# Row norms of two inputs from their turned form, and the first pieces of a two-block model in another order

## The reference, cut to what matters

```python
def rms_norm(x, g):
    xf = x.astype(jnp.float32)
    y = xf * lax.rsqrt(jnp.mean(xf * xf, axis=-1, keepdims=True) + EPS)
    return (y * g.astype(jnp.float32)).astype(x.dtype)

mn = rms_norm(mem, mem_norm_g)
mk, mv = jnp.split(mn @ w_mem_kv, 2, axis=-1)      # 2048 x 1024
xn = rms_norm(h, attn_norm_g)
proj = xn @ w_in                                     # 2048 x 6164
```

## Time and profile before

| what | us |
|---|---|
| three timed runs, median | 2530.12 |
| lowest and highest | 2525.76, 2530.87 |
| the profiled execution, its own time | 2527.56 |
| its span in the trace | 2525.5 |

### The profile page before, as it was taken

The page is one execution under the profiler, slowest core; times in us unless marked ns, Lnnn a source line. Parts: engine busy times, 40 slices in busy tenths (PEclk is TensorE's granted clock), DMA queues, the critical chain, the costliest instruction groups (busy, mean ns, idle before and its releaser), DMA issues.

```text
span 2525.5 us, 31458 instructions
## 1 busy us (share of the span) xinstructions
PE 2480.1 (98%) x12038; PEld 2162.5 (86%) x12038; DVE 1551.1 (61%) x1937; ACT 1231.5 (49%) x1585; POOL 80.2 (3%) x67
## 2 busy tenths in 40 slices
PE   8999999999999999999999999999899999999998
PEld 6888888888888888888888778888788888888887
DVE  6585565665656565666555766766655555555557
ACT  6465554544444444445344545565554444444444
POOL 1032120000000000000000000000000000000000
PEclk9999999999999999999999999999999999999999
DMA  9654656666656566656654446675366666666664
GB/s 363 196 167 134 184 191 210 189 201 196 198 198 199 198 199 199 200 196 221 203 180 133 151 140 200 208 265 184 127 206 200 201 201 199 201 200 200 200 201 136
DMA packets 245128, 490.86 MB, mean 194 GB/s; under 512 B 12016, under 2 KB 13328, under 8 KB 244272
## 3 DMA queue, kind: packets, MB, share of 16 engines
q1 hardware_dynamic: 240576, 470.42, 57.7%
q0 software_dynamic: 3888, 16.01, 1.8%
q10 hardware_dynamic: 576, 3.21, 0.3%
HBM read 487.52 MB, written 2.10 MB: 194 GB/s over the span
## 4 chain that ended last, share of the span: by engine, by line
PE 93%; DVE 3%; ACT 2%; DMA 1%; issue 1%; SPq 0%; DVEq 0%; ACTq 0%
PE ps_a L2384 24%; PE ps_a L2386 24%; PE ps_a L2385 24%; PE ps_b L2386 5%; PE ps_b L2384 5%; PE ps_b L2385 5%; DMA raw<-in_w_mem_kv 1%; DVE wlo L1377 1%; PE ps_b L2710 1%; PE ps_b L2504 1%; PE ps_b L2450 1%; ACT whi L587 1%; PE ps_b L2784 0%; PE ps_b L2774 0%; ACT prob L1043 0%
## 5 line engine op out<-in xcount | busy, mean ns | idle before, releaser
L1377 DVE TENSOR_TENSOR wlo<-raw,whi 128x1024 fp32r<-128x1024 f32 x872 | 1072.2, 1240 | 682.0 <-ACT whi L587 680.2
L587 ACT CAST whi<-raw 128x1024 fp32r<-128x1024 f32 x880 | 911.0, 1045 | 999.9 <-PE ps_a L2386 773.3
L2384 PE MATMUL ps_a<-whi,xhi 128*128 128x512 f32 x1888 | 726.3, 385 | 6.4 <-DVE wlo L1377 3.4
L2385 PE MATMUL ps_a<-wlo,xhi 128*128 128x512 f32 x1888 | 718.1, 380 | 0.0
L2386 PE MATMUL ps_a<-whi,xlo 128*128 128x512 f32 x1888 | 718.1, 380 | 0.0
L2384 PEld LDWEIGHTS ps_a<-whi,xhi 128*128 128x128 f32 x1888 | 358.4, 190 | 62.0 <-issue 8.4
L2386 PEld LDWEIGHTS ps_a<-whi,xlo 128*128 128x128 f32 x1888 | 358.3, 190 | 51.0
L2385 PEld LDWEIGHTS ps_a<-wlo,xhi 128*128 128x128 f32 x1888 | 358.6, 190 | 48.7
L2384 PE MATMUL ps_a<-whi,x2hi 128*128 128x512 f32 x640 | 245.6, 384 | 12.5 <-DVE wlo L1377 12.5
L2385 PE MATMUL ps_a<-wlo,x2hi 128*128 128x512 f32 x640 | 243.2, 380 | 0.0
L2386 PE MATMUL ps_a<-whi,x2lo 128*128 128x512 f32 x640 | 243.2, 380 | 0.0
(11 more groups left out here) (389 smaller groups left out, 2220.2 us busy)
## 6 DMA issues: line engine op xcount, KB each, us to landing
raw<-in_w_in SPq DMA_DIRECT2D x108, 1024.0 KB, 5.4
raw<-in_w_up SPq DMA_DIRECT2D x108, 1024.0 KB, 5.4
raw<-in_w_down SPq DMA_DIRECT2D x108, 1024.0 KB, 5.1
raw<-in_w_gate SPq DMA_DIRECT2D x44, 1024.0 KB, 5.1
raw<-in_w_out SPq DMA_DIRECT2D x16, 1024.0 KB, 5.1
raw<-in_w_mix_out SPq DMA_DIRECT2D x16, 1024.0 KB, 6.1
raw<-in_w_br_attn SPq DMA_DIRECT2D x8, 1024.0 KB, 5.0
raw<-in_w_br_pool SPq DMA_DIRECT2D x8, 1024.0 KB, 5.0
```

What stands on the lines that cost most here:

```text
L587: return nc.scalar.copy(o, i)
L1377: return V.tensor_tensor(wlo[:, q % 4], raw[:, c % SLOTS, 2 * j:2 * j + 2], whi[:, q % 4].bitcast(F32), ALU.subtract).then_inc(lo_done, 1)
L2384: mm(o, x0, m0, start=first and j == 0, stop=False)
L2385: mm(o, x0, m1, start=False, stop=False)
```

## The change

It does these things:

- The rows of `mem`, and the first load of the rows of `x`, are no longer loaded. `h` is loaded once, at L1338 of the kernel before.
- ScalarE squares the turned input in 4 pieces of 128 x 1024 (`feature_squares`) into `feature_sq`, GpSimd adds the 4 pieces and folds the sum twice (`feature_sum`, `feature_fold`: 3 sums of 1024, one of 512, one of 256 elements), and TensorE multiplies each row block of the result by a column of ones (`feature_sums`, two products with one column into bank 4). VectorE reads the sums from PSUM (`row_var`); the root (`row_root`) and the reciprocal (`row_scale`) are placed apart.
- TensorE makes the products with ones for `mem` behind half 10, those for `x` behind half 21.
- GpSimd issues the four `x_t` pieces one by one, each after its part of `mem_t` has been split and squared, and sums between them.
- The first piece of the turned input is 2 feature blocks, not 4; the second chunk of weights comes in two pieces; `gains` is issued by ScalarE.
- VectorE clears 384 columns of `stage_t`, and TensorE multiplies zeros 11 times (128 x 128 by 128 x 256, float32) into `ps_b` ahead of the first product.

The diff, with its outer context lines left out:

```diff
@@ -149,11 +149,10 @@
         ybuf = sb("ybuf", [P, SB, D], at=proj_at)
-        mem_rows = sb("mem_rows", [P, SB, D], at=proj_at)
         mem_t = sb("mem_t", [P, KB, S], at=spots["mix"])
         mem2_t = sb("mem2_t", [P, KB, S], at=spots["mix"])
-        junk = sb("junk", [P, D], at=spots["xkv"])
+        feature_sq = sb("feature_sq", [P, 4, 4 * S], at=proj_at)
         post_gain = sb("post_gain", [P, D], at=proj_at + 16384)
@@ -276,8 +275,10 @@
         hi_done, lo_done, pe_half, evicted = sem("hi_done"), sem("lo_done"), sem("pe_half"), sem("evicted")
-        ld = {n: sem(f"ld_{n}") for n in ("ident", "gains", "base", "gw2", "bias", "cmp", "gain", "first")}
-        gain_sb, table_in = sem("gain_sb"), sem("table_in")
+        ld = {n: sem(f"ld_{n}") for n in ("ident", "gains", "base", "gw2", "bias", "cmp", "gain", "first", "second")}
+        gain_sb, table_in, zeroed = sem("gain_sb"), sem("table_in"), sem("zeroed")
+        feature_squared, feature_summed = sem("feature_squared"), sem("feature_summed")
+        first_flat = sem("first_flat")
         flat_hi, flat_lo = sem("flat_hi"), sem("flat_lo")
@@ -393,11 +394,14 @@
-            sp.dma_start(gains[:], a["gains_t"]).then_inc(ld["gains"], 16)
-            turned_memory(0)
+            sp.dma_start(mem_t[:, 0:2], a["mem_t"][:, 0:2]).then_inc(first_flat, 16)
             sp.dma_start(raw[:, 0, 0:2], rows(w1["memkv"], 0, 2 * P, 0)).then_inc(ld["first"], 16)
+            sp.dma_start(mem_t[:, 2:4], a["mem_t"][:, 2:4]).then_inc(flat_loaded[0][0], 16)
             load(0, rows(w1["memkv"], 2 * P, 2 * P, 0), raw[:, 0, 2:4])
-            for k in range(1, 4):
+            turned_memory(1)
+            sp.dma_start(raw[:, 1, 0:2], rows(w1["memkv"], 4 * P, 2 * P, 0)).then_inc(ld["second"], 16)
+            load(1, rows(w1["memkv"], 6 * P, 2 * P, 0), raw[:, 1, 2:4])
+            for k in range(2, 4):
                 turned_memory(k)
@@ -543,7 +547,7 @@
-        norms = [mem_rows, h, h, h, mix, h, h]
+        norms = [None, None, h, h, mix, h, h]
         norm_loaded = [sem(f"{n}_loaded") for n in ("mem", "x", "mem2")]
@@ -587,6 +591,7 @@
+            act.dma_start(gains[:], a["gains_t"]).then_inc(ld["gains"], 16)
             act.wait_ge(table_in, 1)
@@ -599,6 +604,8 @@
                     act.wait_ge(ld["first"], 16)
+                elif q == 2:
+                    act.wait_ge(ld["second"], 16)
                 else:
@@ -679,15 +686,15 @@
-                if n in (0, 1, 4):
-                    act.wait_ge(norm_loaded[2 if n == 4 else n], 64)
+                if n == 4:
+                    act.wait_ge(norm_loaded[2], 64)
                 elif n == 2:
                     act.wait_ge(post_done, 8 * (n - 4))
-                to = junk if n < 2 else junk_mix if n < 4 else junk3
+                to = junk_mix if n < 4 else junk3
                 src = norms[n]
@@ -764,32 +771,53 @@
                 src, g, x, _ = FLAT[n]
-                act.wait_ge(flat_loaded[n][j // 2], 16)
+                act.wait_ge(first_flat if (n, j) == (0, 0) else flat_loaded[n][j // 2], 16)
                 for kb in range(2 * j, 2 * j + 2):
                 evict(t, 8 * (t + 1), lambda b: mkv[:, b, t * NT:(t + 1) * NT], 0)
+
+            def feature_squares(n, j):
+
+                if n == 1 and j == 0:
+                    act.wait_ge(feature_summed, 5)
+                nc.scalar.activation(feature_sq[:, j], FLAT[n][0][:, 4 * j:4 * j + 4].rearrange("p k s -> p (k s)"), ACT.Square
+                                     ).then_inc(feature_squared, 1)
+
+            def row_root(n):
+
+                act.wait_ge(n_var, n + 1)
+                nc.scalar.activation(s_std, s_var, ACT.Sqrt).then_inc(n_std, 1)
                 some("memkv", j, j + 1)
-            some("memkv", 8, 11)
-            square_sums(0)
-            memkv_out(0)
-            some("memkv", 11, 12)
+                if j > 4:
+                    feature_squares(0, j - 5)
+            some("memkv", 8, 9)
+            feature_squares(0, 3)
+            some("memkv", 9, 12)
             for j in range(4):
                 flat_pair(1, j)
+                if j == 1:
+                    row_root(0)
+                    feature_squares(1, 0)
+                if j == 3:
+                    memkv_out(0)
+                    feature_squares(1, 1)
             for j in range(4):
                     memkv_out(1)
+                if j > 1:
+                    feature_squares(1, j)
             some("in1", 4, 8)
-            square_sums(1)
+            row_root(1)
@@ -1270,13 +1298,28 @@
-            pool.wait_ge(flat_loaded[0][1], 16)
-            load_rows(0, mem_rows, "mem")
-
-            pool.wait_ge(flat_lo, 8)
-            load_flat(1, "x_t")
-            pool.wait_ge(pe_half, 8)
-            load_rows(1, h, "x")
+            def feature_sum(n, j):
+
+                pool.wait_ge(feature_squared, 4 * n + j + 1)
+                if j > 1:
+                    pool.wait_ge(feature_summed, 5 * n + j - 1)
+                nc.gpsimd.tensor_tensor(feature_sq[:, 0], feature_sq[:, 0], feature_sq[:, j], ALU.add).then_inc(feature_summed, 1)
+
+            def feature_fold(n):
+
+                for k, width in enumerate((2 * S, S)):
+                    pool.wait_ge(feature_summed, 5 * n + 3 + k)
+                    nc.gpsimd.tensor_tensor(feature_sq[:, 0, 0:width], feature_sq[:, 0, 0:width], feature_sq[:, 0, width:2 * width],
+                                            ALU.add).then_inc(feature_summed, 1)
+
+            for j in range(4):
+                pool.wait_ge(flat_lo, 2 * j + 2)
+                pool.wait_ge(feature_squared, j + 1)
+                pool.dma_start(x_t[:, 4 * j:4 * j + 4], a["x_t"][:, 4 * j:4 * j + 4]).then_inc(flat_loaded[1][j], 16)
+                if j > 1:
+                    feature_sum(0, j - 1)
+            feature_sum(0, 3)
+            feature_fold(0)
             pool.wait_ge(pe_half, 16)
@@ -1284,6 +1327,9 @@
             pool.dma_start(gw2[:], a["gla_a_w2"]).then_inc(ld["gw2"], 16)
+            for j in range(1, 4):
+                feature_sum(1, j)
+            feature_fold(1)
             pool.dma_start(fbias[:], a["fox_f_b"].rearrange("(r c) -> r c", c=1)).then_inc(ld["gw2"], 16)
@@ -1461,10 +1507,15 @@
+            def row_var(n):
+
+                dve.wait_ge(n_sq, n + 1)
+                V.tensor_scalar(s_var, bank(4)[:, 0:SB] if n < 2 else s_sq, 1.0 / D, EPS, ALU.mult, ALU.add).then_inc(n_var, 1)
+
             def row_scale(n):
-                dve.wait_ge(n_sq, n + 1)
-                V.tensor_scalar(s_var, s_sq, 1.0 / D, EPS, ALU.mult, ALU.add).then_inc(n_var, 1)
+                if n > 1:
+                    row_var(n)
                 dve.wait_ge(n_std, n + 1)
@@ -1575,6 +1626,7 @@
             V.memset(small[:, 252:254], 1.0).then_inc(table_in, 1)
+            V.memset(stage_t[:, 0, 0:S + P], 0.0).then_inc(zeroed, 1)
             dve.wait_ge(ld["gains"], 16)
@@ -1596,17 +1648,20 @@
                 some("memkv", j, j + 1)
-            some("memkv", 8, 11)
-            row_scale(0)
-            some("memkv", 11, 12)
+            some("memkv", 8, 12)
             for j in range(4):
                 flat_pair(1, j)
+                if j == 0:
+                    row_var(0)
+                if j == 2:
+                    row_scale(0)
             for j in range(4):
                 flat_pair(1, 4 + j)
-            some("in1", 4, 8)
-            row_scale(1)
+            some("in1", 4, 7)
+            row_var(1)
+            some("in1", 7, 8)
             def products(x, y, width, out_, blocks=range(SB)):
@@ -1838,6 +1893,8 @@
                 name, k, kn_ = in1_slot(n)
+                if n == 9:
+                    row_scale(1)
                 lo(seg[name][1] + k, chunk=seg[name][0] + k // 2, kn_=kn_)
@@ -1867,7 +1924,7 @@
                 def evict(t, tile):
-                    dve.wait_ge(norm_loaded[1], 128)
+                    dve.wait_ge(norm_loaded[1], 64)
                     for b in range(SB):
@@ -2474,6 +2531,13 @@
+            def feature_sums(n):
+
+                pe.wait_ge(feature_summed, 5 * n + 5)
+                for b in range(SB):
+                    ins = mm(bank(4)[:, b:b + 1], feature_sq[:, 0, b * P:(b + 1) * P], small[:, 252:253], start=True, stop=True)
+                ins.then_inc(n_sq, 1)
+
             def flat_tile(n, name, x):
@@ -2481,10 +2545,16 @@
                     half(q0 + k, (2 * (t0 % 2), 2 * (t0 % 2) + 1), (2 * k, 2 * k + 1), k == 0, k == 7, xh=x[0], xl=x[1])
+                    if (n, k) == (1, 5):
+                        feature_sums(1)
+
+            pe.wait_ge(zeroed, 1)
+            for n in range(11):
+                mm(ps_b[:, 0:S], stage_t[:, 0, S:S + P], stage_t[:, 0, 0:S], start=True, stop=True)
             flat_tile(0, "memkv", (x2hi, x2lo))
-            tile("memkv", 1, x=(x2hi, x2lo))
+            tile("memkv", 1, x=(x2hi, x2lo), behind={2: lambda: feature_sums(0)})
             flat_tile(1, "in1", (xhi, xlo))
```

## The result

The changed kernel takes 2532.69 us in the median of 22 runs, the kernel before 2529.76 in 22 runs beside it. The ratio is 1.0013, 95% interval 1.0007 to 1.0019: slower by 3.3 us, 1.8 to 4.8. I had forecast 2526.5, a gain of 2 us, and a range that ended at 2530.2. The profiled execution took 2533.89, its span 2532.1.

The account below looks back on a forecast made before the run. TensorE, busy 98% of the span, was taken as the bound, its opening bound by what arrives. Gains 1.2 + 1.4 + 2.0 less 0.9 and 1.6 made 2.1 us off 2528.6: 2526.5, range 2523.2 to 2530.2.

Parts of the forecast that it names:

- the start: Opening: less input ahead of the first weights, so the first product stands 1.2 us earlier, bounds 0.5 and 1.6.
- Zeros: Ahead of the first product: zeros raise TensorE's clock, so eight slow first steps go; 1.4 us gained, bounds 0 and 1.4.
- Rows not loaded: Opening transfers: without the rows, weights come sooner and ScalarE's squares are shorter; 2.0 us gained, bounds 1.0 and 2.0.
- both old stalls: TensorE idle before 22.56 and 42.26 us in the kernel before; forecast to go, 0.5 and 1.5 us.
- Products with ones: On TensorE's path: two products per input, 0.45 us an input, 0.9 us lost for both, bounds 0.7 and 1.2.
- the second place: After half 16, GpSimd's 14.8 us against TensorE's six halves, 15.5: no wait, 0.7 us to spare.
- the first place: Up to half 10: TensorE waits 1.6 us for GpSimd's sums; VectorE's subtractions stay under 2.59 us a half.
- The rule I set aside: GpSimd's sums beside VectorE: by whole turns, five subtractions would lengthen 9.6 us to 15.7, a wait of 4.7.
- The long wait for GpSimd: Behind half 10: sums done at 38.9, TensorE through 11 halves at 37.4, so it waits 1.6 us with the signals.
- The rivals: Alternatives to the forecast: short chain 25%, long chain 7%, zeros don't raise the clock 10%, weights don't come sooner 8%.
- The long chain: GpSimd at 4.5 us a sum, chain 16.9: waits of 5.9 and 3.6 us, change -8.4, 2537.0; chance 7%.
- The short chain: GpSimd at 2.56 us a sum, chain 9.6, no wait: gain 3.7, 2524.9; chance 25%.

Follow-up runs that it names:

- the version on VectorE: Changed kernel with GpSimd's sums and folds issued by VectorE between its subtractions; 2524.76 us against 2529.38 for the kernel before, ratio 0.9979.
- the versions without the meetings: Changed kernel with GpSimd's sums cut to one column, or made by VectorE; tail tile starts 4.00 and 3.97 us sooner than in the kernel before.
- the memset run: Changed kernel with each GpSimd sum replaced by a memset of about the same length, sums left out; 2525.49 us against 2529.62 for the kernel before, ratio 0.9980.
- the run without zeros: Changed kernel with the sums made by VectorE and the products with zeros taken out; 2528.28 us against 2529.62 for the kernel before, ratio 0.9993.
- the first experiment: Changed kernel with GpSimd's ten sums cut to one column each; 2525.38 us against 2529.38 for the kernel before, ratio 0.9982.

## Why the prediction was wrong, point by point

**What bounds the kernel, and the start.** Right. First product 8.87 for a forecast 8.95, the first cast at 6.42 for 6.46, the fifth half's at 16.74 for 16.1.

**Zeros.** Right in kind. They took 7.24 us for a forecast 6.4, ended at 8.61, and products were 0.216 apart from the start. That they would count was wrong for this kernel, right for the version on VectorE.

**Rows not loaded.** Right: both old stalls are gone, 2.0 us. The run that loads them again brings the first back, at 2.3 us.

**Products with ones.** Forecast 0.9, measured 0.66 + 0.44. Of the first, some 0.2 is no cost of the products: on the version on VectorE each pair took 0.45, as forecast.

**The step that failed** is a sentence: "VectorE's subtractions, 1.22 alone, took 1.94 and 2.26 beside GpSimd's work; that is still under 2.59 a half." I took two partly covered subtractions for the price of a covered one. It was 3.4 to 3.7, above the 2.59, and the longest stretch of VectorE work in the opening went to waiting. With it went the second place, called hidden with 0.7 us to spare, where a subtraction, two short instructions and the next subtraction sat out the three sums and the first fold. The forecast's sum had VectorE's path at nothing; it measured 2.5 us at the first place, 3.1 at the second, and 1.8 at the lower clock behind it, 7.4 together. Without it the other terms come to 4.7 - 0.9 = 3.8 gained, and the versions without the meetings show 4.0.

**The rule I set aside.** The Trainium skill, SBUF — State Buffer, Who interferes with whom, says that a VectorE instruction with two SBUF inputs and a GpSimd one that reads SBUF exclude each other for a whole instruction. The trace agrees, to 0.02 us at the ends, and the memset run agrees with the rest of it: a GpSimd instruction that only writes held nobody up. I weighed it by durations and found it too strong. The rows of before already bore it out, had I set the ends beside each other. One more row of before, GpSimd's timeline just ahead of the earlier trace rows's product:

```profile
339.36 2.95 POOL L1309 TENSOR_TENSOR mem_o<-mem_o,small 128x512 f32<-128x512 f32 x2 [21.83 <-DVE small L1701]
```

It ends at 342.31. The subtraction that began at 341.46 ended at 343.40, 1.09 later; the gmix product begun at 342.28 was one of two in 6.67, so it ended near 345.62, 2.22 after that; and the subtraction begun at 344.46 ended at 346.72, 1.10 after that. Four ends, whole turns each time. The 3.35 us I took for a sum was 2.24 and one subtraction's turn.

Priced by the rule, five turns would also have come out wrong in place: I added VectorE's turns to GpSimd's chain, and the loss was GpSimd's turns in VectorE's path.

**The long wait for GpSimd** (forecast 1.6 us) hardly existed: the sums were done at 40.00 for a forecast 38.9, but TensorE, late by then, came to them at about 39.9. The chain itself, 27.07 to 40.00, took 12.9 us for a forecast 12.6. That is close because the 3.35 already held a turn of VectorE's; the other side of the same turns was left out.

**The rivals.** None named what happened. The long chain had the right sign, not the mechanism. The short chain's gain, 3.7 us, is what the kernel shows once the meetings are gone; that it lay near is no merit of its reason, a faster GpSimd. The range ended at 2530.2; the median lies 2.5 us above it.

## What to carry to other kernels

Before work goes to GpSimd beside a VectorE that reads two operands from SBUF, count the VectorE instructions that will meet it, and charge each with up to a whole GpSimd instruction, the short ones too. Where VectorE has 1.2 us a period to spare, the sum is cheaper there: it takes half the time and blocks no one. When two engines seem to slow each other, compare the ends of their instructions before fitting a rate.

An earlier start pays only as far as the next bound. Here the opening alone, and the opening with the new sums but the rows loaded again, each gave nothing; with the lighter transfers and the sums on VectorE it gave 0.2%.

## What the runs showed of the hardware

A VectorE instruction can sit out several queued short GpSimd instructions in a row (4.10 us behind four pieces), so cutting the work finer was no cure here. Products with zeros raise TensorE's clock: real products were 0.216 us apart from 8.87 on, where without zeros the first stood 0.43 apart. The slow stretch at the start of a burst differs between executions: eight steps before, eleven in the run without zeros.

After which pauses the clock fell, in the eleven traces that can be read for it, the very start left aside: after each pause from 2.98 us up, and after none of those from 1.33 to 1.54, three or four in a trace (one of 2.21 near 1820 us stands behind one of 3.64, with the clock low already). In between it differs from one execution to the next: the pause of 2.39 or 2.40 near 1515 us was followed by the lower level in seven of eleven traces, the one of 2.27 near 1780 in eight, and single ones of 2.16, 2.19 and 2.47 were not. It also fell without a pause: in all traces near 220 us, among many small products, and in two near 1273 us, right behind 32 products of 32 columns. Before the first experiment I had written of the stretches near 1518 and 1784 that nothing leads up to them; I had overlooked the pauses.

Near 180, 220, 1273, 1515 and 1780 us the time lost at the lower level differs between traces, in steps of 1.7 us. Added up it is 6.8 us in three of them (before, one-column sums, sums on VectorE) and 8.5 or 10.2 in the other eight: up to 3.4 us between traces, all of it behind the opening. The executions without a trace agree. Of 34 of the kernel before, run beside the first experiments, the ten with a mean granted clock of 0.995 took 2527.1 us on the mean, the seven at 0.993 took 2530.5. So most of the spread of 5 us goes with this clock.
